# Where the low half of the down projections' weights is made: a subtraction on VectorE, or a DMA that adds onto the negated high half

## The reference

```python
D_MODEL, SEQ, DEPTH, D_FF = 1024, 256, 4, 2816

def swiglu(x, w_gate, w_up, w_down):
    return (jax.nn.silu(x @ w_gate) * (x @ w_up)) @ w_down

def reference(x, norm_g, final_g, ffn_w_gate, ffn_w_up, ffn_w_down, w_qkv, w_o, ...):
    for i in range(DEPTH):
        x = x + 0.5 * swiglu(rms_norm(x, norm_g[i, 0]), ffn_w_gate[i, 0], ffn_w_up[i, 0], ffn_w_down[i, 0])
        h = rms_norm(x, norm_g[i, 1])
        q, k, v = jnp.split(h @ w_qkv[i], 3, axis=-1)
        ...                     # one of three kinds of attention, 8 heads of 128
        x = x + mix @ w_o[i]
        x = x + 0.5 * swiglu(rms_norm(x, norm_g[i, 2]), ffn_w_gate[i, 1], ffn_w_up[i, 1], ffn_w_down[i, 1])
    return rms_norm(x, final_g)
```

## Time and profile before

| | |
|---|---|
| time, median of 3 executions | 1909.96 us (1909.95 to 1910.46) |
| profiled execution: span | 1908.4 us |
| TensorE busy | 1896.7 us, 99% of the span |
| VectorE busy | 1514.4 us, 79% |
| ScalarE busy | 1055.8 us, 55% |
| GpSimd busy | 41.5 us, 2% |
| DMA moved | 349.17 MB, mean 183 GB/s |

### The profile page before, as it was taken

How to read it: one execution, slowest core, us unless ns; L and a number is a source line. 1 busy time by engine, 2 the same in 40 slices (tenths; PEclk the granted TensorE clock), 3 DMA queues, 4 the chain that set the end, 5 groups by cost and what they waited for, 6 DMA issues and landing times.

```text
span 1908.4 us, 23838 instructions
## 1 busy us (share of the span) xinstructions
PE 1896.7 (99%) x10000; PEld 1626.9 (85%) x10000; DVE 1514.4 (79%) x1421; ACT 1055.8 (55%) x1115; POOL 41.5 (2%) x34
## 2 busy tenths in 40 slices
PE   9999999999999999999999999999999999999998
PEld 8888998888888898888888889988888888998887
DVE  7978667978897788897789876679788987658976
ACT  5655555556555555665555553456556555556553
POOL 0000000000000000100000000000000000000000
PEclk9999999999999999999999999999999999999999
DMA  7555444455544552545554444444555444535443
GB/s 267 208 199 211 165 159 151 189 200 206 189 187 155 219 191 100 212 163 196 220 202 170 177 180 154 173 169 166 199 220 201 165 177 187 201 129 198 177 166 121
DMA packets 49898, 349.17 MB, mean 183 GB/s; under 512 B 6144, under 2 KB 6400, under 8 KB 7936
## 3 DMA queue, kind: packets, MB, share of 16 engines
q1 hardware_dynamic: 49360, 346.54, 48.5%
q10 hardware_dynamic: 432, 1.11, 0.2%
HBM read 346.58 MB, written 1.05 MB: 182 GB/s over the span
## 4 chain that ended last, share of the span: by engine, by line
PE 94%; DVE 4%; ACT 1%; issue 0%; DMA 0%; POOLq 0%; POOL 0%; ACTq 0%; DVEq 0%
PE work L1435 16%; PE work L1304 12%; PE work L1306 12%; PE work L1305 12%; PE acc L1304 10%; PE acc L1306 10%; PE acc L1305 10%; PE work L1433 7%; DVE w_lo L762 2%; PE acc L1348 1%; PE work L1438 1%; PE work L1481 1%; ACT w_hi L465 0%; PE work L1682 0%; PE work L1648 0%
## 5 line engine op out<-in xcount | busy, mean ns | idle before, releaser
L762 DVE TENSOR_TENSOR w_lo<-raw,w_hi 128x2048 fp32r<-128x2048 f32 x311 | 708.1, 2286 | 74.6 <-ACT w_hi L465 72.0
L465 ACT ACTIVATE w_hi<-raw 128x2048 fp32r<-128x2048 f32 x311 | 586.5, 1908 | 92.2 <-DMA raw<-stream_dram 92.2
L1435 PE MATMUL work<-xn,w_hi 128*128 128x512 f32 x1280 | 450.7, 397 | 0.0
L1304 PE MATMUL acc<-w_hi,m_hi 128*128 128x512 f32 x824 | 324.9, 394 | 0.0
L1306 PE MATMUL acc<-w_hi,m_lo 128*128 128x512 f32 x824 | 321.1, 390 | 0.0
L1305 PE MATMUL acc<-w_lo,m_hi 128*128 128x512 f32 x824 | 321.0, 390 | 0.0
L1433 PE MATMUL work<-xn,w_lo 128*128 128x256 f32 x1120 | 314.7, 281 | 0.0
L1435 PEld LDWEIGHTS work<-xn,w_hi 128*128 128x128 f32 x1280 | 234.0, 188 | 44.7 <-issue 0.2
L1433 PEld LDWEIGHTS work<-xn,w_lo 128*128 128x128 f32 x1120 | 211.3, 189 | 7.0
L1306 PEld LDWEIGHTS acc<-w_hi,m_lo 128*128 128x128 f32 x824 | 154.6, 188 | 32.9
L1305 PEld LDWEIGHTS acc<-w_lo,m_hi 128*128 128x128 f32 x824 | 154.9, 188 | 31.4
(11 more groups left out here) (223 smaller groups left out, 2678.3 us busy)
## 6 DMA issues: line engine op xcount, KB each, us to landing
raw<-stream_dram SPq DMA_DIRECT2D x311, 1024.0 KB, 4.9
extra<-stream_dram SPq DMA_DIRECT2D x16, 1024.0 KB, 7.7
x<-x_dram SPq DMA_DIRECT2D x2, 512.0 KB, 8.2
raw<-stream_dram ACTq DMA_DIRECT2D x2, 512.0 KB, 7.8
cst<-consts_dram SPq DMA_DIRECT2D x1, 832.0 KB, 6.8
out_dram<-x SPq DMA_DIRECT2D x3, 256.0 KB, 2.4
final_gain<-final_gain_dram SPq DMA_DIRECT2D x1, 512.0 KB, 6.8
out_dram<-wide SPq DMA_DIRECT2D x1, 256.0 KB, 2.8
```

The lines of the kernel that those rows point to most:

```text
L465: nc.scalar.activation(w_hi[:, c % RING, :], raw_at(place), ACT.Copy).then_inc(hi_ready, 1)
L762: nc.vector.tensor_tensor(w_lo[:, c % RING, :], raw_at(place), w_hi[:, c % RING, :].bitcast(F32), ALU.subtract).then_inc(lo_ready, 1)
L1304: nc.tensor.matmul(dst, a_hi, b_hi, start=start, stop=False, skip_group_check=skip)
L1435: ins = nc.tensor.matmul(bank, hi, xn[:, k].rearrange("p h t -> p (h t)"), start=k == 0, stop=k == DT - 1, skip_group_check=True)
```

## The change

It concerns the 88 down chunks (8 FFNs of 11), called `ADDED`. Their low part is no longer VectorE's subtraction. Instead:

1. right after the copy into `w_hi`, ScalarE reads `raw` again and writes the negated rounded value into `w_lo`, with a scale of -1 (L502 of the new kernel), counting `negative_ready`;
2. GpSimd waits for that count and issues a DMA which reads the same 1 MB chunk from HBM a second time and adds it onto `w_lo` (`accum_op=ALU.add`, L474), so that `w_lo` becomes raw minus high;
3. TensorE waits for the completion of that DMA (one of three semaphores `added_ready`) in place of `lo_ready`.

The `raw` buffer is handed back to SyncE's loads at `negative_ready` and no longer at `lo_ready`. `lo_ready` counts only the chunks that are still subtracted, hence `subtracted(c)`.

```diff
 SUMS, EXTRA = RAW, RAW + 1
+ADDING = 3
+
+
+def added_chunks():
+
+    found = [c0 + w for _, _, c0, att, _ in phases() if not att for w, (what, _) in enumerate(FFN_ORDER) if what == "down"]
+    assert all(b - a >= RING for a, b in zip(found, found[ADDING:]))
+    return found
+
+
+ADDED = added_chunks()
+
+
+def subtracted(c):
+
+    return c + 1 - sum(a <= c for a in ADDED)
...
-                             ("lo", c0 + order.index(("t3", j)) + 1) if load == "b12" else ("lo", w + 1))
+                             ("lo", subtracted(c0 + order.index(("t3", j)))) if load == "b12" else
+                             ("negative", ADDED.index(w) + 1) if w in ADDED else ("lo", subtracted(w)))
...
+        def low_ready(eng, c):
+
+            if c in ADDED:
+                at = ADDED.index(c)
+                eng.wait_ge(added_ready[at % ADDING], 16 * (at // ADDING + 1))
+            else:
+                eng.wait_ge(lo_ready, subtracted(c))
...
             for n in range(NORMS - 1):
                 pool.wait_ge(mean_ready, n + 1)
...
+                if n % 3 != 1:
+                    for _ in range(UNITS):
+                        pool.wait_ge(negative_ready, added + 1)
+                        pool.dma_start(w_lo[:, ADDED[added] % RING, :], stream[AGAIN[added]],
+                                       accum_op=ALU.add).then_inc(added_ready[added % ADDING], 16)
+                        added += 1
...
                 slot_free(act, c)
                 nc.scalar.activation(w_hi[:, c % RING, :], raw_at(place), ACT.Copy).then_inc(hi_ready, 1)
+                if c in ADDED:
+                    nc.scalar.activation(w_lo[:, c % RING, :], raw_at(place), ACT.Copy,
+                                         scale=-1.0).then_inc(negative_ready, 1)
...
             def split_to(c):
                 while split[0] <= min(c, CHUNKS - 1):
-                    lo(split[0])
+                    if split[0] not in ADDED:
+                        lo(split[0])
                     split[0] += 1
...
                 def unit_down(s):
                     u, c = f * UNITS + s, c0 + FFN_ORDER.index(("down", s))
-                    pe.wait_ge(lo_ready, c + 1)
+                    low_ready(pe, c)
                     pe.wait_ge(h_split, u + 1)
                     return contract_pair(c, u % 2 * 2, s == 0)
```

More of the change, by code:

```diff
@@ L124 @@
 SUMS, EXTRA = RAW, RAW + 1
+ADDING = 3
[6 more added lines that the diff above has]
+    return c + 1 - sum(a <= c for a in ADDED)
 def plan():
-    uses, loads, users, places = [], [], [], {}
+    uses, loads, users, places, again = [], [], [], {}, []
     for layer, n, c0, att, no in phases():
@@ L146, in plan @@
                 places[load] = r % RAW, r // RAW + 1
+                if w in ADDED:
+                    again.append(len(loads))
                 loads.append((load, layer, n % 3, j, r % RAW, users[r - RAW] if r >= RAW else None))
                 users.append(("form", len(FORMS) * p + (3 if load == "b11" else 4)) if load in ("b11", "b21") else
-                             ("lo", c0 + order.index(("t3", j)) + 1) if load == "b12" else ("lo", w + 1))
+                             ("lo", subtracted(c0 + order.index(("t3", j)))) if load == "b12" else
+                             ("negative", ADDED.index(w) + 1) if w in ADDED else ("lo", subtracted(w)))
             if what == "t1":
@@ L153, in plan @@
                               ("gu", (no * len(PLAIN) + TURNED) * TB) if earlier < 0 else
-                              ("lo", c0 + order.index(("b22", SEVEN[earlier])) + 1)))
-    return uses, loads
-USES, LOADS = plan()
+                              ("lo", subtracted(c0 + order.index(("b22", SEVEN[earlier]))))))
+    return uses, loads, again
+USES, LOADS, AGAIN = plan()
 def trunk(nc, stream, x_in, gains, consts, lam_in, subln_in, wf_in, bf_in, final_in, out):
@@ L234, in trunk @@
         lo_ready = sem("lo_ready")
+        negative_ready, added_ready = sem("negative_ready"), [sem(f"added_ready{i}") for i in range(ADDING)]
         top_used = sem("top_used")
@@ L399, in load @@
                 if free is not None:
-                    sp.wait_ge({"lo": lo_ready, "form": form_ready, "gu": gu_psum}[free[0]], free[1])
+                    sp.wait_ge({"lo": lo_ready, "form": form_ready, "gu": gu_psum, "negative": negative_ready}[free[0]], free[1])
                 sp.dma_start(raw_at(place), stream[i]).then_inc(b22_loaded if place == EXTRA else raw_loaded[place], 16)
@@ L432, in _ @@
             pool.wait_ge(const_ready, 1)
+            added = 0
             for n in range(NORMS - 1):
@@ L780, in form @@
                     dve.wait_ge(form_ready, len(FORMS) * p + 2)
-                    dve.wait_ge(lo_ready, q + PAIR_ORDER.index("t1") + 1)
+                    dve.wait_ge(lo_ready, subtracted(q + PAIR_ORDER.index("t1")))
                     ins = nc.vector.tensor_tensor(raw_at(SUMS), b12, b11, ALU.add)
                 else:
-                    dve.wait_ge(lo_ready, q + PAIR_ORDER.index("t2") + 1)
+                    dve.wait_ge(lo_ready, subtracted(q + PAIR_ORDER.index("t2")))
                     ins = nc.vector.tensor_tensor(raw_at(SUMS), b21, raw_at(SUMS), ALU.subtract)
@@ L1402, in very_first_step @@
                         gate_up_hi(u, tb, c0, (2, 3))
-                    pe.wait_ge(lo_ready, 1)
+                    low_ready(pe, 0)
                     gate_up_rest(u, 0, c0, (2, 3))
@@ L1409, in very_first_step @@
                         gate_up_hi(u, tb, c0 + 1, bottom)
-                    pe.wait_ge(lo_ready, 2)
+                    low_ready(pe, 1)
                     for tb in range(TB):
@@ L1417, in first_step @@
                     turn_part(n, 2)
-                    pe.wait_ge(lo_ready, c0 + 1)
+                    low_ready(pe, c0)
                     pe.wait_ge(xg_ready, BANKS * n + 1)
@@ L1496, in turned_step @@
                         hidden(s - 1)
-                    pe.wait_ge(lo_ready, c + 2)
+                    low_ready(pe, c + 1)
                     for tb in range(TB):
```

## The result

The changed kernel takes 2163.67 us (median of 4 executions, 2161.27 to 2166.45) against 1910.18 us of the kernel before in the same comparison: a ratio of 1.1328, 95% interval 1.1312 to 1.1344. It is slower by 253 us. The forecast was 2060 us with a range of 1930 to 2200: the direction, the place and the range held, but the loss is 253 us where the sum said 150.

A forecast was written before the change was run, and what follows sets the result against it. TensorE was taken as the bound, busy 1896.7 of 1908.4 us. Down stalls of 131 us, 3 for the first down 0 and 16 for the clock made 150; with 1.6 us around the span, 2060 us, range 1930 to 2200.

The forecast's parts named there:

- VectorE's relief: 88 subtractions leave VectorE, 201 us of busy time; worth 0 to 4 us, taken as 0.
- the cover named: Behind down 3's negation, VectorE no longer subtracts ahead of t4 and b22: cost nothing; without that up to 31 us.
- The rooms: From negation's end to first matmul: 5.0 us at downs 3 and 7, 6.4 at 5 and 9, 8.1 at 4 and 8.
- L: Time from negation's end to the DMA's landing: 10.5 us at downs 3 and 7, 9.1 at downs 5 and 9.
- The price of two reads: Each adding DMA reads two operands: 5.6 us for the bytes plus 2.1 for issue and completion, 7.7 us alone.
- I take half of each, since the addition starts first: At downs 3, 7, 5 and 9, loads sharing the DMA engines cost the addition half of up to 5.6 or 2.8 us.
- The clock: Granted clock falls after long TensorE stalls: 1 us each for 16 stalls, 16 us, from bounds of 0 to 2.5.
- The hidden case: Every addition lands within 5.0 us of its negation's end, so no down stalls: 1910 us; chance 6%.
- the faster case: VectorE's lighter work brings other low parts earlier and TensorE's small waits vanish: at most 4 us, 1906 us; chance 2%.
- the free second read: The second read costs nothing and loads little; only downs 3 and 7 stall, 1.3 us each: 1931 us; rival's chance 20%.
- slow addition: Landing takes 14 us through slow GpSimd issue or adder; downs 1, 2, 3, 5, 7, 9 stall: 2265 us; chance 17%.
- the prediction's own signs: In the changed profile: landing 8 to 11 us, longest wait near 5; 8 us or waits at downs 0 to 2 mean slow addition.

The follow-up runs named there:

- run 8: Changed kernel with only downs 1, 2 and 6 of each FFN added by DMA, the others subtracted on VectorE: 1920.35 us, ratio 1.0051.
- Run 4: Kernel before plus the 88 negations on ScalarE; VectorE adds `raw` onto them instead of subtracting, no DMA from GpSimd: 1977.99 us, ratio 1.0357.
- run 2: Changed kernel with downs 3, 5, 7 and 9 subtracted on VectorE again, the other seven per FFN still added by DMA: 2040.88 us, ratio 1.0681.
- run 1: Changed kernel with GpSimd's DMA copying the chunk plainly instead of adding it, so the low part is wrong: 1951.13 us, ratio 1.0214.
- run 5: Changed kernel with a down chunk's `raw` buffer handed back to the loads one subtraction later, not at the negation: 2126.89 us, ratio 1.1133.
- run 9: Changed kernel with only downs 3 and 7 added by DMA, all other low parts subtracted on VectorE: 2023.28 us, ratio 1.0589.
- runs 9 and 10: Only downs 3 and 7 added by DMA, without (2023.28 us) and with (1992.71 us) 16 zero matmuls ahead of TensorE's wait at each.

## Why the prediction was right, and where its sum was not

- **TensorE bounds, so VectorE's relief is worth nothing: shown.** VectorE was relieved by 185 us (1514.4 to 1329.6) in the changed kernel and by 51 us in run 8, and neither became faster. The small waits for VectorE's results that TensorE has in the kernel before (1.0, 0.5, 0.5 and 0.3 us) stand unchanged in both.
- **Negations put at nothing: right here, and the cover named was the true one.** Run 4 takes the cover away: 67.7 us. The prediction gave up to 31 us for that, 1.91 us at 16 places; the wait rows show 28 places, and 17 us of busy time, 7 of them clock.
- **Downs 3, 5, 7, 9 stall, the others don't: right for the changed kernel.** The rooms were right; that of downs 4 and 8 was measured as 8.3 us against 8.1. That they hide behind the stall ahead of them was said, and run 2 shows it. Down 0 was wrong in all eight FFNs: it stalls 0.7 to 2.4 us in seven of them, and 7.0 us in the first where 2.9 were forecast. Its room in the seven was indeed more than down 1's, some 13 us; what was off is L, 14 us there: GpSimd, busy with the norm until then, issues 0.66 us behind the negation, and two loads are issued some 0.9 and 0.5 us ahead of it.
- **The price of two reads: right.** 5.3 us of engine time per chunk against the forecast's 5.6, and run 1 shows that without the addition most of the loss is gone. The addition alone in the engines was put at 7.7 us; run 5 has 7.9 us, and the last FFN's down 9 in the changed kernel, where no load is left, 8.0. That the doubling comes from the read and not from the adding itself is argued: no run separates them. The rule of the Trainium skill, from "Collectives: The Full Stack", section "The bandwidth ceiling: the fold count and why AG ≠ RS ≠ AR", that an add has two source reads and half the rate, agrees with this trace in size (5.3 against 2.7 us). The estimate of 6.8 us worked out from the Trainium skill, "DMA: Bandwidth & Descriptors", section "Anatomy of one DMA", was too low: no addition of the changed kernel landed before 8.0 us, the median is 11.7.
- **L at downs 3 and 7: 10.5 us forecast, 9.7 measured.** The addition alone has 0.3 us of waking GpSimd and 7.9 us to landing, so the two loads behind it cost about 1.5 us where 2.8 were taken. The stalls are 4.5 us in place of 5.5, 71.4 us in place of 88.
- **L at downs 5 and 9: 9.1 us forecast, 12.1 measured. This is the first term that was mis-sized.** The step that failed is "I take half of each, since the addition starts first". It does not start first: the negation which lets GpSimd issue the addition also frees `raw` for SyncE's load, and SyncE is 0.27 us quicker. The load goes wholly ahead and costs its full 2.8 us: the first packet comes 4.4 instead of 1.57 us behind the issue, and from the first packet on the two additions take about the same (7.8 us at down 3, 7.3 at down 5, 6.4 alone in run 5). Together the loads cost about 3.9 us here where 1.4 were taken. Run 5 turns the order and the stall shrinks with it. The 16 stalls are 79.9 us in place of 43.
- **The clock: 16 us forecast, 68 of the 79 us more busy time measured. This is the largest miss.** The prediction counted "16 stalls" and "1 us" each, out of its own bounds of 0 and 2.5. Since downs 5 and 9 stalled just as long, it was 33 falls: 31 at the four downs, two at downs 0, one of them behind a stall of 2.4 us only. They cost 2.1 us each, in run 9 2.4 us, or 1.9 us of time by runs 9 and 10. The trace of the kernel before shows such a fall only at its very end, where no matmul follows; so how long the clock stays down after a stall could not be read there, and my 1 us had no row behind it. The 11 us of busy time that are left lie outside the low stretches; run 1 has 15.3 us more busy time with hardly any fall, so they are no matter of the clock.
- Stalls at downs 3, 5, 7, 9: 151 us against 131. Down 0: 16 against 3. Clock: 68 against 16, and 11 us of other busy time that the sum did not have. With some 4 us of smaller gaps and rounding this is the 251 us of the span against 150. That 151 is so near 131 is in part luck: the two halves missed in opposite ways (71 against 88, 80 against 43).
- **Rivals.** The hidden case and the faster case are out, as is the free second read. The "slow addition" (L of 14 us) was half right in its median of landings, 11.7 us, but its reason was not: neither GpSimd's issue (0.29 us from the negation's end to its start, but for downs 0) nor a rate below two reads is slow; what is slow is the load ahead. By the prediction's own signs (waits at downs 0 to 2, or one of 8 us) the waits at down 0 would have meant this rival, and the median of landings lies above its 8 to 11 us; the longest wait was 7.0 us. That sign was badly chosen, since down 0 waits for loads ahead and for GpSimd, not for a slow adder.

Left open: whether the second read or the adding takes the double engine time; why a load issued just ahead goes wholly first, while loads issued behind share; and 10 us of busy time in run 4 and 11 us in the changed kernel outside the low clock.

## What to carry to other kernels

A transfer that comes in place of an engine's work has two numbers, its length and the room at *each* use; at a kernel whose bound engine never waits, only the places where length exceeds room matter, and a stall that hides a later one must be taken away together with it. Look at what the same event sets free: a load released by the instruction that triggers a transfer can be issued ahead of it and then takes its whole turn first. And where the bound engine is TensorE, a stall of over 4 us cost its length and about 2 us more of half-speed matmuls here, which no wait row shows, and now and then a stall of 2 us did too; compare busy times for the same instructions.

## What the runs showed of the hardware

- A DMA of 1 MB that adds onto SBUF takes 5.3 us of all 16 engines, a plain one from the same queue 2.7 us. It landed 8.0 / 11.7 / 16.4 us after its issue (min, median, max), a plain one 5.0 / 8.0 / 11.7. With no load beside it until 7.1 us or later, it took 7.9 us (run 5, downs 5 and 9).
- GpSimd's own instruction for it is longer too, 0.86 us against 0.53 for the plain copy.
- A load of 1 MB issued 0.27 us ahead on SyncE's queue kept the addition's first packet back for 4.4 us, against 1.57 us where the loads were issued 1.2 us behind. In both cases the earlier transfer ran alone at first. The later loads began some 5.3 us behind the addition's instruction and shared the engines with it from then on.
- After 4.4 us without a matmul the granted clock was 0.50 for the next 3 us, after 5.2 us for the next 5; in run 4 it was 0.50 behind four waits of 1.9 us, with TensorE busy throughout the low stretch; sixteen matmuls of zeros ahead of the wait kept it at 0.999 in the mean.
